# One attention stage, its slots in another order: page copies, narrow weights, masks and the next pair's product

## What is computed

```
def stick_breaking(q, k, v, bias, q_pos, k_pos):
    z = jnp.einsum('nqhd,nkhd->nhqk', q, k).astype(jnp.float32) * (C_HEAD_DIM ** -0.5) + bias.astype(jnp.float32)[None, :, None, None]
    mask = (k_pos[None, :] < q_pos[:, None])[None, None]
    log_beta = jax.nn.log_sigmoid(z)
    log_1m = jnp.where(mask, jax.nn.log_sigmoid(-z), 0.0)
    rest = lax.cumsum(log_1m, axis=3, reverse=True) - log_1m
    w = jnp.where(mask, jnp.exp(log_beta + rest), 0.0)
    return jnp.einsum('nhqk,nkhd->nqhd', w, v.astype(jnp.float32)).astype(q.dtype)
```

## Time and profile before

| what | us |
|---|---|
| median of 3 runs (3548.02 to 3550.63) | 3548.84 |
| the profiled execution | 3551.58 |
| its span, first to last instruction | 3549.8 |
| PE busy in the span (86%) | 3062.0 |
| DVE busy (46%) | 1620.3 |
| ACT busy (25%) | 882.1 |
| POOL busy (26%) | 938.6 |

### The profile page before, as it was taken

The page is one execution under the profiler, slowest core; times in us unless marked ns, Lnnn a source line. Parts: engine busy times, 40 slices in busy tenths (PEclk is TensorE's granted clock), DMA queues, the critical chain, the costliest instruction groups (busy, mean ns, idle before and its releaser), DMA issues.

```text
span 3549.8 us, 52658 instructions
## 1 busy us (share of the span) xinstructions
PE 3062.0 (86%) x20085; PEld 2820.6 (79%) x20085; DVE 1620.3 (46%) x1899; ACT 882.1 (25%) x1505; POOL 938.6 (26%) x461
## 2 busy tenths in 40 slices
PE   7888886959999999967888888888686999999994
PEld 6787885949999999957666666666586999999994
DVE  3554544662332212363665666556675233221236
ACT  3233231031101101023454444545403100100102
POOL 3221211323343333332121121111032333333330
PEclk9898987979999999978898998989797999999997
DMA  3010110101111111102333233332210111111111
GB/s 100 25 35 25 30 36 19 36 18 47 42 48 41 47 42 47 34 25 86 94 99 100 90 120 90 96 102 90 79 47 18 47 42 47 41 42 47 47 36 49
DMA packets 311740, 195.87 MB, mean 55 GB/s; under 512 B 12842, under 2 KB 309495, under 8 KB 311610
## 3 DMA queue, kind: packets, MB, share of 16 engines
q1 hardware_dynamic: 302522, 189.63, 17.8%
q10 hardware_dynamic: 9088, 4.52, 0.4%
HBM read 178.70 MB, written 15.40 MB: 55 GB/s over the span
## 4 chain that ended last, share of the span: by engine, by line
PE 76%; DVE 13%; ACT 5%; issue 4%; DMA 0%; POOL 0%; SPq 0%; ACTq 0%; DVEq 0%; POOLq 0%
PE bank L1403 61%; DVE E L1194 3%; PE bank L1654 2%; PE bank L1416 2%; PE bank L1630 2%; DVE LS L1312 2%; PE bank L1567 2%; PE bank L1642 1%; DVE R L1307 1%; PE bank L1581 1%; DVE R L1318 1%; ACT WTK L757 1%; DVE KTP L1215 1%; ACT E L788 1%; PE bank L1610 1%
## 5 line engine op out<-in xcount | busy, mean ns | idle before, releaser
L1403 PE MATMUL bank<-XH,WH 128*128 128x352 f32 x3264 | 1087.2, 333 | 36.2 <-ACT Q L644 10.0
L1403 PE MATMUL bank<-XH,WL 128*128 128x352 f32 x3264 | 1066.2, 327 | 0.0
L1403 PE MATMUL bank<-XL,WH 128*128 128x352 f32 x3264 | 1065.1, 326 | 0.0
L560 POOL TENSOR_TENSOR WH<-RAW,zero 128x1024 fp32r<-128x1024 f32 (+1 forms) x204 | 393.2, 1927 | 2400.1 <-PE bank L1403 2291.4
L1403 PEld LDWEIGHTS bank<-XH,WH 128*128 128x128 f32 x3264 | 630.2, 193 | 61.8 <-issue 47.9
L1403 PEld LDWEIGHTS bank<-XH,WL 128*128 128x128 f32 x3264 | 631.7, 194 | 0.0
L1403 PEld LDWEIGHTS bank<-XL,WH 128*128 128x128 f32 x3264 | 628.3, 192 | 0.0
L1403 PE MATMUL bank<-HH,WH 128*128 128x352 f32 x1440 | 473.5, 329 | 56.9 <-DVE HL L1353 32.3
L563 POOL TENSOR_TENSOR WL<-RAW,WH 128x1024 fp32r<-128x1024 f32 (+1 forms) x204 | 512.6, 2513 | 16.0
L1403 PE MATMUL bank<-HH,WL 128*128 128x352 f32 x1440 | 469.1, 326 | 0.0
L1403 PE MATMUL bank<-HL,WH 128*128 128x352 f32 x1440 | 468.3, 325 | 0.0
(11 more groups left out here) (277 smaller groups left out, 3162.8 us busy)
## 6 DMA issues: line engine op xcount, KB each, us to landing
PG<-in_cache_k_dram SPq DMA_DIRECT2D x256, 128.0 KB, 2.2
PG<-in_cache_v_dram SPq DMA_DIRECT2D x256, 128.0 KB, 2.2
RAW<-in_ffn_w_gate_dram SPq DMA_DIRECT2D x44, 512.0 KB, 3.8
RAW<-in_ffn_w_up_dram SPq DMA_DIRECT2D x44, 512.0 KB, 3.8
RAW<-in_ffn_w_down_dram SPq DMA_DIRECT2D x32, 512.0 KB, 3.8
RAW<-in_c_w_in_dram SPq DMA_DIRECT2D x28, 512.0 KB, 4.6
RAW<-in_ab_w_in_dram SPq DMA_DIRECT2D x24, 512.0 KB, 3.9
RAW<-in_ffn_w_down_dram SPq DMA_DIRECT2D x16, 384.0 KB, 3.3
```

The lines of the kernel that those rows point to most:

```text
L560: nc.gpsimd.tensor_tensor(WH[slot][:, 0:kb, :], RAW[slot][:, 0:kb, :], zero[:].to_broadcast([P, kb, P]), ALU.add).then_inc(w_split, 1)
L1403: last = t.matmul(bank[:, 0:CW], w[slot][:, k, :], x[:, k, CH[c]], start=n == 0, stop=n == 3 * kb - 1)
```

## The change

No instruction of the computation is added or dropped; the lists are put in another order, and a few waits go with it.

- PE, slot 0: the product for the next pair stands ahead of the second logits, behind two turns of values; it was behind the second logits.
- PE, slots 1 to 8: the product stands behind the turn of the slot before's weights and ahead of its values; it was ahead of the turn. The whole product (all eight blocks of 128 rows) goes there (`next_products`).
- The samples' queries S go to bank 4, so that the product behind them does not wait for their copy.
- ACT: in slot 0 the item is copied first, and the turned tokens are copied between the heads' `log1p_exp`. In other wide slots the turned weights of the narrow slot before are copied between the heads. The item is copied behind the turned weights.
- DVE: `exponent` is cut into `suffix_sums` (scan) and `exponent` (subtract), and three of the places for page copies are between them: behind the first scan, behind the first subtract, behind the second scan.
- V_SPOTS moves page values to the places behind the first logits and behind the product.
- Masks: POOL makes the second pair of splits ahead of WTN's mask; PE, ACT and DVE no longer wait for all masks at the start, and WTN is turned in slot 0 of pair 0.

```diff
--- before.py
+++ after.py
-        V_SPOTS = [(), (1, 0, 1, 0, 1)] + [(0, 0, 1, 0, 1)] * 5 + [(1, 0, 1, 0, 1), ()]
+        V_SPOTS = [(), (0, 0, 1, 1, 1), (1, 0, 0, 1, 0), (0, 0, 0, 1, 1), (1, 0, 0, 1, 0), (0, 0, 0, 1, 1), (1, 0, 0, 1, 0),
+                   (0, 0, 1, 1, 1), ()]
...
+                split_pair("c", KD, 1)
                 for q in range(2):
                     rows = WTN[:].rearrange("c (j q r) -> c j q r", j=4, q=2)[:, :, q, :]
...
-                splits("c", len(C_TILE) // 2, KD, 1)
+                splits("c", len(C_TILE) // 2, KD, 2)
...
             def attention_act():
-                act.wait_ge(at_pool, 14)
...
                         if p < NPOS:
-                            for h in range(2):
-                                log1p_exp(hp, p, h)
-                        for x in items:
-                            item(*x, banks[7])
+                            log1p_exp(hp, p, 0)
                         if p == 0:
                             value_tokens(hp, 2)
                             for b in range(3 * odd):
                                 sample_turned(hp, b)
+                        elif p < NPOS and WIDE[p]:
+                            weights_turned(hp, p - 1, 0)
+                        if p < NPOS:
+                            log1p_exp(hp, p, 1)
                         if p == 1:
                             for b in range(3):
                                 key_tokens(hp, b)
+                        if p == NPOS or not WIDE[p]:
+                            weights_turned(hp, p - 1, 0)
                         if p >= 1:
-                            weights_turned(hp, p - 1, 0)
+                            for x in items:
+                                item(*x, banks[4 if x[0] == "S" else 7])
                         if p < NPOS:
                             weights(hp, p, 0)
...
             def attention_dve():
-                dve.wait_ge(at_pool, 14)
...
                             copies()
+                            suffix_sums(hp, p, 0)
+                            copies()
                             exponent(hp, p, 0)
                             copies()
+                            suffix_sums(hp, p, 1)
+                            copies()
                             exponent(hp, p, 1)
-                            copies()
-                            copies()
+                            if hp + p == 0:
+                                new_token_cap()
...
-                pe.wait_ge(at_pool, 14)
-                t.transpose(banks[4][:, 0:NS], WTN[:], ident[0:NS, 0:NS]).then_inc(cap_mm, 1)
+
+                def new_token_cap():
+                    pe.wait_ge(at_pool, 14)
+                    freed(ITEMS[9])
+                    t.transpose(banks[6][:, 0:NS], WTN[:], ident[0:NS, 0:NS]).then_inc(cap_mm, 1)
...
+                def next_products(items, k0, k1):
+                    for x in items:
+                        if x[0] == "S":
+                            if k0 == 0:
+                                item(*x, banks[4])
+                            continue
+                        if k0 == 0:
+                            freed([y for y in ITEMS[:ITEMS.index(x)] if y[0] != "S"][-1])
+                        item(*x, banks[7], k0, k1)
...
+                        if p == 0:
+                            value_tokens(hp, 1)
+                            next_products(items, 0, KD)
                         fill()
                         if p < NPOS and WIDE[p]:
                             logits(hp, p, 1)
-                        if p == 0:
-                            value_tokens(hp, 1)
                         fill()
-                        for x in items:
-                            freed(ITEMS[ITEMS.index(x) - 1])
-                            item(*x, banks[7])
                         if p == 0:
                             value_tokens(hp, 2)
+                            if hp == 0:
+                                new_token_cap()
                             for b in range(2 * odd):
                                 sample_turn(hp, b)
...
                         if p >= 1:
                             turn(hp, p - 1, 0)
+                            next_products(items, 0, KD)
                         fill()
```

More of the change, by code:

```diff
@@ L724, in queries @@
                     e = hp % 2
+                    if hp < 2:
+                        act.wait_ge(at_pool, 3)
                     for h in range(2):
@@ L848, in pair @@
                                 sample_log1p_exp(d)
+                        if p == 0:
+                            for x in items:
+                                item(*x, banks[7])
                         if p < NPOS:
-                            for h in range(2):
-                                log1p_exp(hp, p, h)
-                        for x in items:
-                            item(*x, banks[7])
+                            log1p_exp(hp, p, 0)
                         if p == 0:
@@ L1161, in attention_dve @@
                 v.tensor_reduce(rowbias[:], rowtmp[:, 0:16].rearrange("p (d e) -> p d e", e=4), AX, ALU.add).then_inc(row_own, 1)
-                dve.wait_ge(cap_mm, 1)
-                v.tensor_copy(CAPQ[:], banks[4][:, 0:NS]).then_inc(cap_ready, 1)
+                def new_token_cap():
+                    dve.wait_ge(cap_mm, 1)
+                    v.tensor_copy(CAPQ[:], banks[6][:, 0:NS]).then_inc(cap_ready, 1)
                 def q_rest(hp, c, bank):
@@ L1181, in logits_in @@
                         if part == 0:
+                            if hp + p == 0:
+                                dve.wait_ge(at_pool, 4)
                             if p >= 2:
@@ L1187, in logits_in, with suffix_sums @@
                             v.tensor_scalar(z, bank, bias, ZCAP, ALU.add, ALU.min).then_inc(z_ev, 1)
-                def exponent(hp, p, h):
-                    u, w = 2 * NPOS * hp + 2 * p + h + 1, WIDTH[p]
-                    z, e = ZS[WIDE[p]][h], ES[h]
+                def suffix_sums(hp, p, h):
+                    u, w, e = 2 * NPOS * hp + 2 * p + h + 1, WIDTH[p], ES[h]
                     dve.wait_ge(e_ln, u)
@@ L1195, in exponent @@
                                          ALU.mult, ALU.add).then_inc(suffix, 1)
+                def exponent(hp, p, h):
+                    u, w, z, e = 2 * NPOS * hp + 2 * p + h + 1, WIDTH[p], ZS[WIDE[p]][h], ES[h]
                     dve.wait_ge(suffix, u)
@@ L1510, in attention_pe, with new_token_cap, item @@
                 pe.wait_ge(ln_cent, 6)
-                pe.wait_ge(at_pool, 14)
-                t.transpose(banks[4][:, 0:NS], WTN[:], ident[0:NS, 0:NS]).then_inc(cap_mm, 1)
+                def new_token_cap():
+                    pe.wait_ge(at_pool, 14)
+                    freed(ITEMS[9])
+                    t.transpose(banks[6][:, 0:NS], WTN[:], ident[0:NS, 0:NS]).then_inc(cap_mm, 1)
                 def freed(x):
                     pe.wait_ge(q_lo if x[0] == "Q" else c_free, FREED[x])
-                def item(kind, c, hp, bank):
+                def item(kind, c, hp, bank, k0=0, k1=KD):
                     n = C_TILE[kind, hp]
-                    if c == 0 or kind == "S" or kind == "Q" and c == 2:
+                    if k0 == 0 and (c == 0 or kind == "S" or kind == "Q" and c == 2):
                         pe.wait_ge(w_split, 2 * n + 5)
                     if kind != "S":
-                        product(n % 2, KD, c, XH, XL, bank)
+                        for k in range(k0, k1):
+                            for m, (w, x) in enumerate(((WH, XH), (WL, XH), (WH, XL))):
+                                last = t.matmul(bank[:, 0:CW], w[n % 2][:, k, :], x[:, k, CH[c]],
+                                                start=k == 0 and m == 0, stop=k == KD - 1 and m == 2)
+                        if k1 == KD:
+                            last.then_inc(d_mm, 1)
                         return
@@ L1561, in turn_pages @@
                     if s == 0:
-                        pe.wait_ge(cap_ready, 1)
                         if hp:
@@ L1649, in values @@
                         pe.wait_ge(po_ev, NPOS * hp + p)
+                    if part == 0 and hp + p == 0:
+                        pe.wait_ge(cap_ready, 1)
                     pe.wait_ge(t_ev, TURN[hp, p, part, 1] + 1)
```

## The result

The changed kernel takes 3568.77 us (median, 3566.68 to 3573.66), the kernel before 3548.43 beside it: ratio 1.0057, 95% interval 1.0041 to 1.0073, some 20 us slower. The profiled execution took 3568.55 us (span 3566.8), 17.0 more than that of before. The forecast was 3567, and slower.

What follows compares the result with a forecast made beforehand. The attention stage was taken as bound by PE's own work plus some 17 us a pair waiting on a chain round the engines. Odd +13.5, even +7.6, entry −3.5 and last pair +0.5 gave +18: 3567 us, range 3543 to 3587.

Steps and rivals of the forecast that it cites:

- Entry: Stage start: PE no longer waits for POOL's masks, so the third product ends 4.1 us earlier; taken as −3.5 us.
- Odd slots 0 and 1: Odd pairs' first block: softmax left uncovered, +4.2 us, and a product after a sparse stretch, +1.7; +5.9 in all.
- it ends at T 6.3: Slot 0's moved product in odd pairs ends 6.3 us after the block's first logits, so second logits end at T 7.3.
- Odd slots 6 to 8: Odd pairs' last block: bank 4 frees the product from ACT, and two products cover the softmax; 28.6 against 33.1, −4.5 us.
- Even slots 0 to 3: Even pairs: slots 0 and 1 +4.3 us, slots 2 and 3 −1.4 us, each including +1.7 for the clock.
- the clock term: Products of slots 1 and 3 follow sparse stretches and run slower: +1.7 us each, 14 products in seven pairs.
- Even slots 6 to 8: Even pairs' last block: slot 7's product uncovers two gaps of some 2 us, less the last copy; +1.0 us.
- Last pair: No product to move; ACT's 1.7 us of copies stand against 3.5 us of scan and subtract; +0.5 us.
- A: Rival: PE's clock stays up, the 14 charges of 1.7 us go; 3543 us, no measurable change; chance 0.17.
- B: Rival: softmax chains end before PE asks, so removed waits alone count; 3514 us; chance 0.10.
- C: Rival: products of slots 5 and 7 in even pairs also run slow, 14 us more; 3581 us; chance 0.13.
- D: Rival: splits delay DVE by whole instructions in odd slots 3, 7 and even 5, some 6 us; 3573 us; chance 0.10.

Runs made afterwards that it cites:

- x5_even: Changed kernel with slots 6 to 8 of even pairs back in the old order on PE, ACT and DVE: 3549.31 us, −1.5 against the kernel before.
- c_fill: Changed kernel plus 22 unneeded turns on PE ahead of slot 0's product in odd pairs: 3563.20 us, ratio 1.0032 to the kernel before.
- z2_s7: Samples' queries back in bank 7, against a mix of old and changed orders by blocks (3503.82 us): 3511.40 us.
- z1_dve: DVE's old order in all slots of even pairs, against a mix of old and changed orders by blocks (3503.82 us): 3523.83 us.
- x6_last: Changed kernel with ACT's old order in the last pair: 3570.34 us, +19.5 against the kernel before.
- x3_odd1: Changed kernel with slot 1's product of odd pairs back ahead of the turns: +13.9 us against the kernel before.
- x4_odd01: Changed kernel with odd pairs' products of slots 0 and 1, slot 1's V_SPOTS and slot 0's ACT order as before: +0.7 us against the kernel before.
- x7_even01: Changed kernel with slots 0 and 1 of even pairs back in the old order on PE, ACT and DVE: 3551.38 us, +0.6 against the kernel before.

## Why the prediction came out

**Entry, right.** −3.5 forecast, −3.6 in the profile, −4.7 (−0.7 to −7.5) alone. The first product starts at 1598.19 against 1609.52, 11.3 us earlier (11 said).

**Odd slots 0 and 1, sign right, size too small (+5.9 against +9.5 on average).** The step that failed is "it ends at T 6.3". I moved the product past the wait that it already had, for bank 7, freed by QL, and did not ask when QL is ready. It was ready 0.7 us late by the order of before (x5_even); the even pairs' new order made that 3.3 us. Of the increase, 1.7 us are the samples' scan and subtract, slowed as POOL's split now began ahead of the scan, and the rest is the scan's later start; this is read from rows, as no run delays the split alone. In pairs 1 and 3 the product behind the wait also ran at a lower clock; with the wait filled it did not (c_fill). With both gone the block takes 33.6 us, near the 32.5 that the steps gave. The uncovered softmax was there as described: 2.62 us ahead of a turn of the samples' weights, for ACT's copy of the new values, and 3.52 ahead of the third turn of keys, where I had said 5.7 in one piece and named over 4 as the sign.

**Odd slots 2 to 5, nearly right.** Slot 3's turns of weights wait 2.77 and 4.10 us for the exponential (5 or more said), slot 5's 1.99 (2 said); +2.1 against +3.1, and −0.4 against 0.

**Odd slots 6 to 8, right, too small.** −6.2 on average against −4.5. The bank of S alone is worth 3.2 (z2_s7); I had counted its wait, not the clock of the product behind it. That clock does not follow the bank alone: in pair 1 the product behind S took 5.22 us with no wait ahead of it, 3.93 in pair 3, and these slots took 28.1 us against 26.5 in the other two pairs.

**Even slots 0 to 3, the clock term wrong.** I charged 1.7 us for the products of slots 1 and 3, as if they had run at 4.04 us before. In the even pairs they were the slow ones already: the 5.83 of the earlier trace rows is slot 1's product in pair 2, and slot 3's, on the same chain, is this:

```profile
1933.57 5.66 PE bank L1403 x24
```

After, these two take 4.15 and 4.08 us, so the term has the wrong sign there. Of the 14 times 1.7 us, those in odd slots 1 and 3 came, somewhat smaller (5.30 and 5.16 against 4.04 for slot 1 before); those in even pairs did not. With no charge the steps give +2.6 and −3.1 against +2.5 and −2.3 measured; with the 1.6 us credited, +1.0 and −4.7, so the steps themselves promised some 2 us more than came. Over the stage PE's rows of products come to 277.0 us, before to 283.6: no net loss, though the stage's mean clock fell from 0.90 to 0.87.

**Even slots 4 and 5: too small,** −3.1 against −2.0; z1_dve puts most of it on DVE's page copies, where I had also named copies of weights.

**Even slots 6 to 8: +2.7 against +1.0.** Here the change works against itself:

```profile
1996.69 0.69 DVE L1231 COPY KTP<-bank 128x512 f32<-128x512 f32 x1 [5.24 <-PE bank L1608]
1997.30 1.22 DVE L1206 TENSOR_TENSOR_SCAN E<-ones,E 128x512 f32<-128x512 f32 x1
...
2006.22 1.06 ACT L760 ACTIVATE WTK<-bank 128x512 f32<-128x512 f32 x2
...
2007.43 1.09 PE L1683 MATMUL bank<-WTK,VTOK 128*64 128x128 f32 x16 [1.65 <-ACT WTK L760]
```

DVE's second scan of slot 7 stands behind a page copy that waits 5.24 us for PE, busy with the product. And the last copies of weights wait on ACT behind the samples' logarithm, so the product does not cover them, as I had said it would. x5_even takes these slots back to 33, and through the split the odd ones behind them.

**Last pair: +6.5 against +0.5.** I looked at ACT's order, worth 0.7 at most (x6_last). What I left out is that the second logits wait for DVE behind the samples' softmax, 4.59 us where it was 2.46. The rest is open.

**The sum** was right because errors met: even pairs came out 8.4 us better than forecast, the odd ones 1.4 and the last pair 6.0 worse. The closeness of 3567 to 3568.77 was luck. That it came out slower was luck in part too: the main reason, uncovered softmax in slots 0 to 3, is there (the product of slot 1 put back gives 4 us in a block, x3_odd1), but x5_even leaves all of it in place and is level with the kernel before (−1.5 us), as are x4_odd01 and x7_even01, which take back a part of it. So the 20 us also needed slots 6 to 8 of the even pairs and what they set off in the next pair, which the forecast had at +4.0 and at nothing.

**Rivals.** A: the products' clock did hold up in even pairs, but the time went elsewhere. B did not come: the turns of weights wait 34.5 us. C came in one place of eight: slot 7's product of pair 6 takes 5.04 us on the chain, the others of slots 5 and 7 in even pairs 3.8 to 4.1. D: its mechanism is there (below), its price of 6 us is not to be seen in the blocks it named, of which even slots 4 and 5 got faster; it acted at a border that I had not looked at.

## What to carry to other kernels

When an instruction is moved ahead, list every semaphore that it already waits for and ask at what time each is ready in the new place; a wait that cost nothing where it stood is the first thing to go wrong. Read a reordering block by block and keep each block's better order: the times of single blocks added up within 2 us (−47 against −45), where the whole change lost 20 and its parts gained 47. Work that a moved step triggers on another engine, here POOL's split, is part of the move.

## What the runs showed of the hardware

A scan or subtract on DVE and a split on POOL wait for each other by whole instructions. In the changed kernel the scan at 1770.58 ends at 1774.19: POOL's part ends at 1771.98, and 2.21 us later the scan is done. POOL's next, from 1772.06, runs to 1776.34, 2.15 us after the scan's end; the subtract, from 1774.23, ends 1.11 us after that. The profile counts the blocked time as busy. The Trainium skill, page "SBUF — State Buffer", section "SBUF: two separate sides", says this of the port pair that VectorE, in an instruction with two inputs in SBUF, and GpSimd share: whichever starts first holds it for its whole instruction. The rows here agree, 2.36 us for the scan that came first and 3.61 for the one that came 0.49 us late.

The clock of a product depends on more than the wait ahead of it: after the same 3.3 us of idle time it took 4.08 and 6.84 us (x7_even01), and after 1.4 us it took 5.65 (z2_s7). Work that nobody needs, 22 turns in that wait in each of three pairs, made the kernel 8 us faster.
